# Fifteen RMS-norm roots by one ACTIVATE from PSUM, in a transformer stack on one core

## The reference, cut to what matters

```python
def rms_norm(t, g, eps=1e-6):
    t32 = t.astype(jnp.float32)
    t32 = t32 * lax.rsqrt(jnp.mean(t32 * t32, axis=-1, keepdims=True) + eps)
    return t32.astype(t.dtype) * g.astype(t.dtype)

for i in range(2):                       # first block
    f = swiglu(rms_norm(h, g), w_gu, w_down);   h = h + 0.5 * rms_norm(f, g)
    m = short_conv(rms_norm(h, g)) if i == 0 else diff_attention(rms_norm(h, g))
    h = h + rms_norm(m, g)
    f = swiglu(rms_norm(h, g), w_gu, w_down);   h = h + 0.5 * rms_norm(f, g)
# second block: mixers (gated linear attention and dilated attention), then relu^2 MLP
h = h + mixers(rmsnorm(h)) @ w_out
h = h + square(relu(rmsnorm(h) @ w_ff1)) @ w_ff2
return rmsnorm(h)
```

## Time and profile before

| | |
|---|---|
| runs | 1401.14, 1402.42, 1403.07 us; median 1402.42 |
| profiled execution | 1401.28 us; its span from first to last instruction 1399.5 us |
| busy | PE 1358.9 us (97%), weight loads 1331.9, DVE 891.9 (64%), ACT 648.1 (46%) |
| granted TensorE clock | 0.995 of full speed |
| ACT table loads | 11, of 1283 ns each |
| L923 mean on DVE | 15 times, median 441 ns |
| L510 and L514, Ln on ACT | 6 and 9 times, median 487 and 431 ns |
| L516, Exp on ACT | 15 times, median 431 ns |
| L928, L930, L933, Newton on DVE | 15 times each, medians 433, 441, 441 ns |
| stages (start to start) | gu0/dn0 0 to 211 us, conv to 320, gu1/dn1 to 528, gu2/dn2 to 735, qkv/attn_out to 879, gu3/dn3 to 1075, mixers to 1200, ff1/ff2 to the end |

### The profile page before, as it was taken

How to read it: one execution, slowest core, us unless ns; L and a number is a source line. 1 busy time by engine, 2 the same in 40 slices (tenths; PEclk the granted TensorE clock), 3 DMA queues, 4 the chain that set the end, 5 groups by cost and what they waited for, 6 DMA issues and landing times.

```text
span 1399.5 us, 26677 instructions
## 1 busy us (share of the span) xinstructions
PE 1358.9 (97%) x11002; PEld 1331.9 (95%) x11002; DVE 891.9 (64%) x1317; ACT 648.1 (46%) x925; POOL 13.5 (1%) x27
## 2 busy tenths in 40 slices
PE   7999999999999999999998999899999999999997
PEld 7999999998999999999998988899999999899996
DVE  6666547758666547665547887866655767777543
ACT  6444435446444535444435565644445445544332
POOL 0000000000000000000000000000001000000000
PEclk9999999999999999999999999999999999999998
DMA  7555543334545533555444223355655513455550
GB/s 282 179 180 202 189 180 136 136 126 146 179 166 202 204 121 126 175 180 212 179 180 146 83 84 121 125 190 191 218 193 192 196 62 121 142 188 181 181 181 30
DMA packets 30829, 227.67 MB, mean 163 GB/s; under 512 B 3520, under 2 KB 5888, under 8 KB 6816
## 3 DMA queue, kind: packets, MB, share of 16 engines
q1 hardware_dynamic: 29312, 223.56, 44.9%
q0 software_dynamic: 720, 1.82, 0.4%
q10 hardware_dynamic: 720, 1.19, 0.3%
HBM read 225.49 MB, written 1.06 MB: 162 GB/s over the span
## 4 chain that ended last, share of the span: by engine, by line
PE 86%; DVE 9%; ACT 4%; issue 1%; DMA 0%; SPq 0%; DVEq 0%; ACTq 0%
PE ps L1536 25%; PE ps L1538 24%; PE ps L1537 24%; DVE w_lo L903 3%; ACT w_hi L484 2%; PE ps L1582 1%; PE ps L1577 1%; PE ps L1578 1%; PE ps L1611 1%; PE ps L1602 1%; PE ps L1600 1%; ACT s_exp L651 1%; PE ps L1552 1%; DVE small L1135 0%; DMA w_raw<-w_gu 0%
## 5 line engine op out<-in xcount | busy, mean ns | idle before, releaser
L903 DVE TENSOR_TENSOR w_lo<-w_raw,w_hi 128x2048 fp32r<-128x2048 f32 (+2 forms) x182 | 468.2, 2572 | 212.6 <-ACT w_hi L484 212.6
L484 ACT ACTIVATE w_hi<-w_raw 128x2048 fp32r<-128x2048 f32 (+2 forms) x182 | 389.6, 2141 | 384.0 <-PE ps L1538 371.9
L1536 PE MATMUL ps<-x_hi,w_hi 128*128 128x272 f32 (+1 forms) x1952 | 561.9, 288 | 0.4 <-DVE hid L1437 0.4
L1538 PE MATMUL ps<-x_hi,w_lo 128*128 128x272 f32 (+1 forms) x1952 | 559.1, 286 | 0.0
L1537 PE MATMUL ps<-x_lo,w_hi 128*128 128x272 f32 (+1 forms) x1952 | 557.5, 286 | 0.0
L1536 PEld LDWEIGHTS ps<-x_hi,w_hi 128*128 128x128 f32 x1952 | 368.4, 189 | 5.2 <-issue 4.8
L1538 PEld LDWEIGHTS ps<-x_hi,w_lo 128*128 128x128 f32 x1952 | 368.5, 189 | 0.0
L1537 PEld LDWEIGHTS ps<-x_lo,w_hi 128*128 128x128 f32 x1952 | 368.1, 189 | 0.1
L1536 PE MATMUL ps<-hid_hi,w_hi 128*128 128x272 f32 (+1 forms) x960 | 274.7, 286 | 0.2 <-DVE w_lo L903 0.2
L1538 PE MATMUL ps<-hid_hi,w_lo 128*128 128x272 f32 (+1 forms) x960 | 274.4, 286 | 0.0
L1537 PE MATMUL ps<-hid_lo,w_hi 128*128 128x272 f32 (+1 forms) x960 | 273.5, 285 | 0.0
(11 more groups left out here) (285 smaller groups left out, 1373.0 us busy)
## 6 DMA issues: line engine op xcount, KB each, us to landing
w_raw<-w_gu SPq DMA_DIRECT2D x87, 1024.0 KB, 4.9
w_raw<-w_dn SPq DMA_DIRECT2D x32, 1408.0 KB, 6.0
w_raw<-w_ff SPq DMA_DIRECT2D x32, 1024.0 KB, 4.9
w_raw<-w_conv_in SPq DMA_DIRECT2D x8, 1536.0 KB, 6.4
w_raw<-w_qkv SPq DMA_DIRECT2D x8, 1536.0 KB, 6.4
w_raw<-w_mix_in SPq DMA_DIRECT2D x8, 1536.0 KB, 6.5
w_raw<-w_conv_out SPq DMA_DIRECT2D x4, 1024.0 KB, 4.9
w_raw<-w_attn_out SPq DMA_DIRECT2D x4, 1024.0 KB, 4.9
```

Of the source, the lines that this page charges most:

```text
L484: act.activation(w_hi[j % SPLIT][:, 0:width], w_raw[j][:, 0:width], ACT.Copy).then_inc(hi_ready, 1)
L903: dve.tensor_tensor(w_lo[j % SPLIT][:, 0:width], w_raw[j][:, 0:width], w_hi[j % SPLIT][:, 0:width].bitcast(F32), ALU.subtract).then_inc(lo ...
L1536: pe.matmul(out_ap, w_hi[slot][:, cols], hi(k), start=first, stop=False)
L1538: mm = pe.matmul(out_ap, w_lo[slot][:, cols], hi(k), start=False, stop=last)
```

## The change

The root becomes one ACTIVATE, Abs_reciprocal_sqrt with scale 1/1024 and bias eps, which reads the sum in PSUM, for pre-norms and post-norms alike. DVE forms no mean: Newton's first operation takes the factor -0.5/1024, and its second reads the sum in PSUM and adds 1024 * eps to it. The buffer ms and two semaphores go. The new function lies in a table set of its own, so the places where tables are loaded change. The diff, cut to its core:

```diff
-            def root(s, c0, from_psum=False):
-                if from_psum:
-                    act.wait_ge(sumsq_summed, s // 2 + 1)
-                    act.activation(r0[:, c0:T], ps[:, SUM + 1, c0:T], ACT.Ln, scale=1.0 / D, bias=eps_col)\
-                       .then_inc(ln_ready, 1)
-                else:
-                    act.wait_ge(ms_ready, s + 1)
-                    act.activation(r0[:, c0:T], ms[:, c0:T], ACT.Ln).then_inc(ln_ready, 1)
-                act.wait_ge(ln_ready, s + 1)
-                act.activation(r0[:, c0:T], r0[:, c0:T], ACT.Exp, scale=-0.5).then_inc(r0_ready, 1)
+            def root(s, c0, bank, summed, count):
+                act.wait_ge(summed, count)
+                act.activation(r0[:, c0:T], ps[:, bank, c0:T], ACT.Abs_reciprocal_sqrt, scale=1.0 / D, bias=eps_col)\
+                   .then_inc(r0_ready, 1)
...
-            act.preload_act_table_set(LN_EXP_SET)
+            act.preload_act_table(ACT.Abs_reciprocal_sqrt)
             act.wait_ge(eps_ready, 2)
...
-                root(s, c0)
+                root(s, c0, SUM, h_sq_summed, u + 1)
...
                     hidden(f"gu{f}", f, c0)
-                    act.preload_act_table_set(LN_EXP_SET)
+                    act.preload_act_table(ACT.Abs_reciprocal_sqrt)
                     out_projection(f"dn{f}", DN_N, 1, u, c0, post)
...
                     c0 = META
+                    act.preload_act_table_set(LN_EXP_SET)
                     heads()
+                    act.preload_act_table(ACT.Abs_reciprocal_sqrt)
                     out_squares(u)
-                root(s, c0, from_psum=True)
+                root(s, c0, SUM + 1, sumsq_summed, u + 1)
...
-            root(s, META)
+            root(s, META, SUM, h_sq_summed, 7)
             s += 1
+            act.preload_act_table_set(LN_EXP_SET)
             mixers()
             pre_parts(7, META, "mlp_norm")
+            act.preload_act_table(ACT.Abs_reciprocal_sqrt)
             third_hi("ff1")
...
-            def mean(c0, bank, summed, count, eps):
-                dve.wait_ge(summed, count)
-                dve.tensor_scalar(ms[:, c0:T], ps[:, bank, c0:T], 1.0 / D, eps, ALU.mult, ALU.add).then_inc(ms_ready, 1)
-            def root(s, c0):
+            def root(s, c0, bank):
                 dve.wait_ge(r0_ready, s + 1)
-                dve.tensor_tensor(rstd[:, c0:T], r0[:, c0:T], r0[:, c0:T], ALU.mult).then_inc(newton, 1)
+                dve.scalar_tensor_tensor(out=rstd[:, c0:T], in0=r0[:, c0:T], scalar=-0.5 / D, in1=r0[:, c0:T],
+                                         op0=ALU.mult, op1=ALU.mult).then_inc(newton, 1)
                 dve.wait_ge(newton, 2 * s + 1)
-                dve.scalar_tensor_tensor(out=rstd[:, c0:T], in0=rstd[:, c0:T], scalar=-0.5, in1=ms[:, c0:T],
-                                         op0=ALU.mult, op1=ALU.mult).then_inc(newton, 1)
+                dve.scalar_tensor_tensor(out=rstd[:, c0:T], in0=ps[:, bank, c0:T], scalar=D * NORM_EPS, in1=rstd[:, c0:T],
+                                         op0=ALU.add, op1=ALU.mult).then_inc(newton, 1)
...
                 elif name != "qkv":
                     next_lo(name, TRI_N, 0, 0)
-                mean(c0, SUM, h_sq_summed, q + 1, NORM_EPS)
                 if f is not None:
                     third_lo(f, name, 1)
...
-                mean(c0, SUM + 1, ln_ready, s + 1, NORM_EPS)
-                root(s, c0)
+                root(s, c0, SUM + 1)
```

More of the change, by code:

```diff
@@ L167, in two_blocks @@
         ones = sb("ones", [P, P])
-        ms = sb("ms", [P, T])
         r0 = sb("r0", [P, T])
@@ L282, in two_blocks @@
             sem("h_sq_ready"), sem("h_sq_grouped"), sem("h_sq_copied"), sem("h_sq_summed"), sem("sumsq_summed"))
-        ms_ready, ln_ready, r0_ready, newton, rstd_ready = (
-            sem("ms_ready"), sem("ln_ready"), sem("r0_ready"), sem("newton"), sem("rstd_ready"))
+        r0_ready, newton, rstd_ready = sem("r0_ready"), sem("newton"), sem("rstd_ready")
         x_hi_ready, x_lo_ready = sem("x_hi_ready"), sem("x_lo_ready")
@@ L882, in _ @@
             low_inputs()
-            root(s, META)
+            root(s, META, SUM, h_sq_summed, 7)
             s += 1
+            act.preload_act_table_set(LN_EXP_SET)
             mixers()
             pre_parts(7, META, "mlp_norm")
+            act.preload_act_table(ACT.Abs_reciprocal_sqrt)
             third_hi("ff1")
-            root(s, META)
+            root(s, META, SUM, h_sq_summed, 8)
             s += 1
@@ L895, in _ @@
                 h_square(8, m, META)
-            root(s, META)
+            root(s, META, SUM, h_sq_summed, 10)
         @block.vector
@@ L969, in pre_root @@
                     next_lo(name, TRI_N, 0, 0)
-                root(s, c0)
+                root(s, c0, SUM)
             def post_norm(u, s, c0, factor, gain):
-                mean(c0, SUM + 1, ln_ready, s + 1, NORM_EPS)
-                root(s, c0)
+                root(s, c0, SUM + 1)
                 for k in range(KD + 2):
@@ L1518, in _ @@
             dve.wait_ge(h_ready, 8 * KD)
-            mean(META, SUM, h_sq_summed, 10, NORM_EPS)
-            root(s, META)
+            root(s, META, SUM)
             for k in range(KD):
```

## The result

The changed kernel takes 1394.1 us (median of 4 runs, 1393.26 to 1395.16) against 1402.51 us for the kernel before: ratio 0.9944, interval 0.993 to 0.9958. By the ratio it is faster by about 7.9 us (the medians lie 8.4 apart), where 4.5 had been forecast; the range, 1396.0 to 1400.1, does not hold it. The profiled execution of after took 1395.16 us, the slowest of its four, with a span of 1393.4 us; that of before had taken 1401.28 us, near the low end of its runs, with a span of 1399.5. So the two traces lie 6.1 us apart and the medians 8.4: part of the difference depends on which execution was caught.

The account below looks back on a forecast made before the run. PE's dense matmuls bound the kernel (86% of the span), so only PE's waits can pay. 2.3 + 0.34 + 0.85 + 0.71 + 0.35 = 4.55 us; 4.5 off the median 1402.42 gives 1397.9 us, range 1396.0 to 1400.1.

Parts of the forecast that it names:

- The six post-norms: Seams behind post-norms: Newton and the weight split start earlier, 0.46 us at five (2.3) and 0.34 us after attention.
- The final norm: Serial mean, Ln and Exp at the kernel's end become one root, so Newton starts 0.85 us earlier.
- qkv and ff1: Two pre-norm openings where DVE's w_lo starts earlier: 0.71 us in qkv, 0.35 us in ff1.
- Table loads: Four more on ACT, 11 to 15, hidden under idle or slack: 0 us; without cover 1.3 us each.
- The rival in which a drain came with each load: At out_squares, load and drain of 2.66 us against 2.14 us idle cost 0.52 us: 1398.4 us, chance 0.05.
- The other six pre-norms I cost at nothing.: Pre-norms outside qkv and ff1: PE's matmuls cover them, gain 0; without cover at most 0.85 us each.
- So the gain should be carried through the stage.: In qkv and the heads: the opening's 0.71 us lasts, since the next heads again wait for k_rot.
- Runs of one kernel lie 1.9 us apart: Scatter used for the odds: 0.05 moved to the middle, giving faster 0.83, same 0.14, slower 0.03.
- more than the sum: In mix_in rstd comes at least 0.85 us earlier and may reach another wait: 5.4 us, 1397.0 us, chance 0.08.

Follow-up runs that it names:

- the doubled operation: Changed kernel with Newton's first operation made twice, one behind the other, in the six post-norms: 1397.7 us, 3.3 above the changed kernel.
- the wait put back: Changed kernel with DVE's wait for the sum put back before the coming block's w_lo in pre_root, without the mean: 1393.96 us.
- the mean put back: Changed kernel with the mean back in the eight pre-norms, the root there reading ms, and ms in its old place: 1398.02 us.
- the warmed pair: Changed kernel and kernel before, both with unread matmuls in five PE waits, the latter also with ms over rstd_sq and 14 more keep-warm matmuls: 1393.59 and 1399.61 us.
- warmed kernel before: Kernel before with unread matmuls in five PE waits: 1400.91 us; with ms over rstd_sq 1400.11; with 14 more keep-warm matmuls after attention too, 1399.61.
- warmed changed kernel: Changed kernel with matmuls whose result nobody reads in five places where PE waits 1.4 us or longer: 1393.59 us, ratio 0.9936 to the kernel before.

## Why the prediction was wrong

Its direction, its mechanisms and its priced terms at the places named were right; the sum was too small because of two terms put at nothing or too low and two things that were not in it. The first items below held, the last four failed.

- **The six post-norms.** Forecast 2.3 + 0.34, found 2.27 + 0.33. The seams are passed on in full, as the doubled operation shows from the other side.
- **The final norm.** 0.85 forecast, 0.84 found.
- **qkv and ff1.** 0.71 and 0.35 forecast, 0.72 and 0.41 found. The reason in qkv, the queue behind the mean, is shown by the wait put back (0.38 us) and by the mean put back (0.70).
- **Table loads.** Cost nothing, as forecast. The rival in which a drain came with each load would need the squares after attention late; the load ran from 865.05 to 866.33 us and they began at 866.95, behind a wait for PE. The Trainium skill's 2.66 us per switch (ScalarE: Activation LUTs, What ACT_TABLE_LOAD costs) is not seen here: next ACTIVATEs stand 1.29 us behind a load's start.
- **"The other six pre-norms I cost at nothing."** The step failed in conv, by 0.25 us. I had read only the list of waits, where a hold this short does not appear. On the timeline of before PE's third block starts right after cv_u, which hangs on rstd:

```profile
236.07 0.43 DVE L1061 TENSOR_TENSOR cv_u<-cv_c,ps 128x272 f32<-128x272 f32 x1
...
236.65 0.36 PE L1536 MATMUL ps<-x_hi,w_hi 128*128 128x272 f32 x1
```

After, cv_u is done 1.4 us before the block starts, and PE goes from its last matmul into the block without a pause. The two warmed traces, which have no stretch at half clock, show the same 0.25 us. The lines of after:

```profile
234.40 0.43 DVE L1052 TENSOR_TENSOR cv_u<-cv_c,ps 128x272 f32<-128x272 f32 x1
...
236.19 0.29 PE L1526 MATMUL ps<-x_hi,w_hi 128*128 128x272 f32 x1
```

- **"So the gain should be carried through the stage."** The 0.71 us of qkv's opening were carried, and about 0.3 us more were gained at the last head, in the warmed pair too, where the clock has no part in it. The two runs that delay that opening again lose more over the whole attention stage than in its opening, 0.6 us for 0.4 and 1.0 for 0.7, but the surplus falls at the fifth head and not at the last; what ties these places to the opening was not followed. In the warmed kernel before, ACT starts the last w_hi of the stage 0.24 us later behind the small root in front of it than in the warmed changed kernel, and w_lo and z_lo follow; why, is open.
- **"Runs of one kernel lie 1.9 us apart", taken for noise that both kernels share.** They don't share it. Much of the scatter is the number of stretches at 1.2 GHz behind PE's waits (the length of the start-up adds up to 1 us), and the changed kernel has fewer that cost time. By medians over all groups of runs, warming removes 2.5 us from the kernel before (1402.1 to 1399.6) and 0.8 us from the changed one (1394.4 to 1393.6), 1.7 us of the gain; by the ratios within each group it removes 2.1 and 1.2, or 0.9 us of the gain. Why the changed kernel has fewer is only in part known. Of the waits of 1.4 us and more, the change shortens two, the one before the first scores (2.76 to 2.06 us) and the one after attention (1.91 to 1.57). At the latter, filling the wait removed the stretch; that 0.35 us less of wait is enough rests on three profiles of warmed kernels, and the doubled Newton operation had 2.03 us of wait there without a stretch. In conv_out PE's wait is 1.93 us in both kernels, yet the stretch was there in all four profiles with a mean in the pre-norms and in two of five unwarmed ones without; why, is open.
- **The buffer ms, which the sum did not mention.** Its going moved all later buffers by 1088 bytes per partition, and that gave 0.9 us. The traces show it from both sides: ms kept in the changed kernel and ms laid over another buffer in the kernel before. Of what ff2's matmuls read, w_hi and w_lo lie ahead of ms and did not move, hid_hi and hid_lo did; which of these two matters was not tried.

Together: 4.57 (forecast 4.55) + 0.25 + 0.3 + 0.9 = 6.0 us, which the warmed pair confirms, and 0.9 to 1.7 us that go with the clock: 6.9 to 7.7 of the 7.9 us. What is missing lies within the scatter of medians of four to eleven runs.

The rival "more than the sum" (1397.0) foresaw the direction of the miss, but named mix_in as the place, where rstd did come 1.05 us early and nothing waited for it.

## What to carry to other kernels

A serial chain of small operations at a seam can be summed from the trace to a few hundredths of a microsecond, and one ACTIVATE fewer there is worth its whole stride. On a PE-bound kernel look also at PE's waits of a microsecond and more, since one may be followed by matmuls at half clock; compare runs with their granted clock beside them, and price scatter by its cause before calling it noise. When a buffer goes or comes, keep the addresses in a control kernel, or the unchanged stages will lend the change a gain that isn't its own.

## What the runs showed of the hardware

PE's pace at full clock depended on where its operands lie: with hid_hi and hid_lo 1088 bytes per partition further down, a matmul of 256 columns in ff2 took 117.8 and not 118.7 ns, in every profile of either layout. The down projections of 272 columns, which read the same two buffers, took 126.1 ns in both layouts, and ff1, whose operands had not moved, showed no difference.

The granted clock fell to its lower level at PE's waits of 1.4 to 2.8 us or within 2 us behind them, in some executions and not in others; matmuls put into those waits removed it. With the earlier waits covered the stretch could come up behind a wait that had been free of it (884 us). What a stretch cost ran from nothing (on keep-warm matmuls, 874 us) to 1.5 us (conv_out, and behind the x_hi wait after attention). The Trainium skill, TensorE: Matmul & The Clock Gate, Part 1, gives this clock 1.2 and 2.4 GHz as its two levels while fewer than three cores of a die are busy, and says that it follows how busy PE has been. The two levels are what the granted clock shows here, 0.5 and 1.0; the 0.225 and 0.126 us between matmuls of 272 columns stand 1.8 to 1.

ACT_TABLE_LOAD took 1283 ns, and wherever work was ready behind it the next ACTIVATE started 1.29 us after the load's start, at 752.16 and 1205.30 us among others.
